# Rounded high and low parts for the query/key norms and the attention scores of a hybrid encoder layer

## The reference

```python
h = rms_norm(x, norm_mix)
proj = h @ w_in                      # fq, fk, fv: 512 columns each, then the other mixers' columns
q = rms_norm(q, q_gain) * (hd ** -0.5)   # per head, over 64 columns
k = rms_norm(k, k_gain)
c = cumsum(log_sigmoid(f_logit))
sc = einsum('bhqd,bhkd->bhqk', q, k) + c[query] - c[key]
p = softmax(where(query >= key, sc, -inf))
o = einsum('bhqk,bhkd->bhqd', p, v)
```

## Time and profile before

| | us |
|---|---|
| median of 3 runs | 872.98 (872.17 to 873.1) |
| the profiled execution | 872.24 |
| its span, first to last instruction | 870.5 |
| PE busy | 840.0 (97%) |
| DVE busy | 579.1 (67%) |
| ACT busy | 475.7 (55%) |

### The profile page before, as it was taken

How to read it: one execution, slowest core, us unless ns; L and a number is a source line. 1 busy time by engine, 2 the same in 40 slices (tenths; PEclk the granted TensorE clock), 3 DMA queues, 4 the chain that set the end, 5 groups by cost and what they waited for, 6 DMA issues and landing times.

```text
span 870.5 us, 11553 instructions
## 1 busy us (share of the span) xinstructions
PE 840.0 (97%) x4188; PEld 673.5 (77%) x4188; DVE 579.1 (67%) x678; ACT 475.7 (55%) x563; POOL 92.2 (11%) x131
## 2 busy tenths in 40 slices
PE   5999999999999989999999999989999999999994
PEld 4777777777877768888888888867888888888883
DVE  5555436766745887324254265788898988889893
ACT  6375445554455242322332332557888788888882
POOL 6510000000000110100000010103112111111001
PEclk9999999999999999999999999999999999999998
DMA  6432012213112031332232494599999999999973
GB/s 213 146 98 72 25 49 98 98 48 98 50 49 97 1 96 49 100 104 97 90 104 97 185 321 164 204 383 347 386 388 369 362 371 377 374 366 352 376 295 49
DMA packets 60173, 164.26 MB, mean 189 GB/s; under 512 B 9592, under 2 KB 10705, under 8 KB 60130
## 3 DMA queue, kind: packets, MB, share of 16 engines
q1 hardware_dynamic: 51504, 145.89, 45.5%
q0 software_dynamic: 4464, 12.66, 6.4%
q10 hardware_dynamic: 4162, 5.13, 1.7%
HBM read 154.16 MB, written 13.11 MB: 192 GB/s over the span
## 4 chain that ended last, share of the span: by engine, by line
PE 90%; DVE 4%; ACT 2%; DMA 1%; issue 1%; POOL 0%; POOLq 0%; DVEq 0%; ACTq 0%
PE bank L1986 26%; PE bank L1988 25%; PE bank L1987 25%; PE bank L2457 1%; PE bank L2108 1%; PE bank L2139 1%; PE bank L2124 1%; DMA xg<-h2rows,tabid 1%; PE bank L2464 1%; PE bank L2096 1%; PE bank L2240 1%; PE bank L2324 1%; PE bank L2190 1%; PE bank L2198 0%; ACT whi L715 0%
## 5 line engine op out<-in xcount | busy, mean ns | idle before, releaser
L737 DVE TENSOR_TENSOR wlo<-mstage,whi 128x2048 fp32r<-128x2048 f32 x95 | 215.5, 2290 | 28.9 <-ACT whi L715 28.8
L715 ACT ACTIVATE whi<-mstage 128x2048 fp32r<-128x2048 f32 x96 | 183.8, 1919 | 25.6 <-PE bank L1988 25.1
L737 DVE TENSOR_TENSOR wlo<-stage,whi 128x2048 fp32r<-128x2048 f32 (+1 forms) x39 | 87.8, 2251 | 96.1 <-ACT whi L715 95.4
L1986 PE MATMUL bank<-hTh,whi 128*128 128x512 f32 x368 | 149.4, 406 | 0.3 <-DVE wlo L1445 0.3
L1988 PE MATMUL bank<-hTh,wlo 128*128 128x512 f32 x368 | 143.7, 390 | 0.0
L1987 PE MATMUL bank<-hTl,whi 128*128 128x512 f32 x368 | 143.4, 390 | 0.0
L715 ACT ACTIVATE whi<-stage 128x2048 fp32r<-128x2048 f32 (+1 forms) x39 | 73.0, 1874 | 75.9 <-PE bank L1988 71.1
L1986 PE MATMUL bank<-whi,xTh 128*128 128x512 f32 (+1 forms) x264 | 104.3, 395 | 2.1 <-DVE xTl L1809 1.1
L1988 PE MATMUL bank<-whi,xTl 128*128 128x512 f32 (+1 forms) x264 | 101.5, 384 | 0.0
L1987 PE MATMUL bank<-wlo,xTh 128*128 128x512 f32 (+1 forms) x264 | 101.2, 383 | 0.0
L1986 PEld LDWEIGHTS bank<-hTh,whi 128*128 128x128 f32 x368 | 69.2, 188 | 17.4 <-issue 2.8
(11 more groups left out here) (383 smaller groups left out, 1333.6 us busy)
## 6 DMA issues: line engine op xcount, KB each, us to landing
mstage<-in_w_exp_gate SPq DMA_DIRECT2D x32, 1024.0 KB, 11.9
mstage<-in_w_exp_up SPq DMA_DIRECT2D x32, 1024.0 KB, 12.0
mstage<-in_w_exp_down SPq DMA_DIRECT2D x32, 1024.0 KB, 12.4
stage<-in_w_in SPq DMA_DIRECT2D x28, 1024.0 KB, 5.0
stage<-in_w_branch SPq DMA_DIRECT2D x6, 1024.0 KB, 5.0
stage<-in_w_out SPq DMA_DIRECT2D x4, 1024.0 KB, 5.1
xin<-in_x SPq DMA_DIRECT2D x4, 512.0 KB, 5.3
x<-in_x SPq DMA_DIRECT2D x4, 512.0 KB, 7.4
```

Of the source, the lines that this page charges most:

```text
L715: nc.scalar.activation(whi_of(u)[:, :, 0:n], source_of(u)[:, :, 0:n], ACT.Copy).then_inc(hi_ready, 1)
L737: nc.vector.tensor_tensor(wlo_of(u)[:, :, 0:n], source_of(u)[:, :, 0:n], whi_of(u)[:, :, 0:n].bitcast(F32), ALU.subtract).then_inc(lo_read ...
L1986: t.matmul(out, lhs[0], rhs[0], start=start, stop=False)
```

## The change

The sums of squares and the scores are made from rounded high and low parts.

1. `square`: ACT, after squaring, also copies the square to a rounded `qsqh`; DVE has a new step that subtracts it from the square (`qsql`) and only then signals `sq_done`. PE multiplies a rounded `blk64r` with both.
2. `parts` m (m = 0 to 7): ACT copies the normed `foxq` or `foxk` to `foxqh` or `foxkh`, DVE subtracts (`foxql`, `foxkl`, in place of the original). Those of the queries stand in the four slots of the second half of block fk, `parts` 4 right behind the last `qscale`, `parts` 5 to 7 in the first three steps of attention.
3. `score`: three matmuls for each head in place of one, in the order high*high, high*low, low*high, each for both heads. The first score of a head pair waits for the key's low part (`ql_done`), the first of all no longer for `qn_done`.
4. POOL makes `blk64r` with one more copy of 128x128. `cum16` moves to another address.

```diff
+    for q in range(4):
+        early.setdefault((1, 1, q), []).append(("parts", q))
...
+                done += [("parts", 4)] if m[0] == 7 else []
...
+        if n < 3:
+            out.append(("parts", 5 + n))
...
+        foxql = at("foxql", 104, [P, 4, T], F32R)
+        foxkl = at("foxkl", 112, [P, 4, T], F32R)
+        foxqh = at("foxqh", 128, [P, 4, T], F32R)
+        foxkh = at("foxkh", 136, [P, 4, T], F32R)
...
-        cum16 = at("cum16", 128, [16, T])
+        cum16 = at("cum16", Z0 + 10, [16, T])
...
+            step(g.tensor_copy(blk64r[:, :], blk64[:, :]))
...
+                elif kind == "parts":
+                    m = it[1]
+                    act.wait_ge(qn_done, m + 1)
+                    step(a.activation((foxqh if m < 4 else foxkh)[:, m % 4, :], (foxq if m < 4 else foxk)[:, m % 4, :],
+                                      ACT.Copy), qh_done, m + 1)
...
-                    step(a.activation(qsq[:, m % 2, :], (foxq if m < 4 else foxk)[:, m % 4, :], ACT.Square),
-                         sq_done, m + 1)
+                    step(a.activation(qsq[:, m % 2, :], (foxq if m < 4 else foxk)[:, m % 4, :], ACT.Square))
+                    step(a.activation(qsqh[:, m % 2, :], qsq[:, m % 2, :], ACT.Copy), sqh_done, m + 1)
...
+                elif kind == "square":
+                    m = it[1]
+                    dve.wait_ge(sqh_done, m + 1)
+                    step(v.tensor_tensor(qsql[:, m % 2, :], qsq[:, m % 2, :], qsqh[:, m % 2, :].bitcast(F32), ALU.subtract),
+                         sq_done, m + 1)
+                elif kind == "parts":
+                    m = it[1]
+                    dve.wait_ge(qh_done, m + 1)
+                    step(v.tensor_tensor((foxql if m < 4 else foxkl)[:, m % 4, :], (foxq if m < 4 else foxk)[:, m % 4, :],
+                                         (foxqh if m < 4 else foxkh)[:, m % 4, :].bitcast(F32), ALU.subtract),
+                         ql_done, m + 1)
...
-                    t.matmul(whole(b), blk64[:, :], qsq[:, m % 2, :], start=True, stop=True).then_inc(full[b], 1)
+                    t.matmul(whole(b), blk64r[:, :], qsqh[:, m % 2, :], start=True, stop=False)
+                    t.matmul(whole(b), blk64r[:, :], qsql[:, m % 2, :], start=False, stop=True).then_inc(full[b], 1)
...
+                    if i == 0:
+                        pe.wait_ge(ql_done, 5 + pr)
                     if n == 0:
-                        pe.wait_ge(qn_done, 8)
                         pe.wait_ge(cuml_done, 2)
-                    for hh, r in enumerate(rows_of):
-                        t.matmul(bank[4 + hh][:, 0:w], foxq[r, pr, i * P:(i + 1) * P], foxk[r, pr, 0:w],
-                                 start=True, stop=False)
+                    for a, b, first in ((foxqh, foxkh, True), (foxqh, foxkl, False), (foxql, foxkh, False)):
+                        for hh, r in enumerate(rows_of):
+                            t.matmul(bank[4 + hh][:, 0:w], a[r, pr, i * P:(i + 1) * P], b[r, pr, 0:w],
+                                     start=first, stop=False)
```

More of the change, by code:

```diff
@@ L445, in build @@
         qsq = at("qsq", Z0, [P, 2, T])
+        qsql = at("qsql", Z0, [P, 2, T], F32R)
+        qsqh = at("qsqh", Z0 + 4, [P, 2, T], F32R)
+        blk64r = at("blk64r", 153, [P, P], F32R)
         qrs = at("qrs", 136, [P, 4, T])
@@ L595, in build @@
             "sq_done", "qrs_done", "qn_done", "min_done", "prob_done", "pv_done", "oAh_done", "tanh_done"))
+        sqh_done = sem("sqh_done")
+        qh_done, ql_done = sem("qh_done"), sem("ql_done")
         sel_done, cumh_done, cuml_done, acsm_done = (sem(n) for n in ("sel_done", "cumh_done", "cuml_done", "acsm_done"))
```

## The result

The change made the kernel slower. The median is 876.76 us (875.65 to 877.56) against 873.04 us for the kernel before in the same job (872.17 to 873.44): +3.7 us, a ratio of 1.0045 (95% interval 1.0035 to 1.0055). The profiled execution took 877.27, its span 875.5 us, 5.0 more than before.

A forecast was written before the change was run, and what follows sets the result against it. PE bounds the kernel, but ACT and DVE hand-overs set its pace up to the first score. Waits 7.1, checks -3.8 and scores -1.9 gave +1.4 on 872.98: 874.4 us, range 871.6 to 877.4.

The forecast's parts named there:

- rival A: The new wait before the first score draws a half-clock stretch of 3.4 us: +1.7, 876.1 us; chance 0.20.
- What bounds the kernel: PE, busy 97% of the span; from 43 to 93.7 us ACT and DVE hand-overs make PE's own savings buy nothing.
- First check: First product for the norm's sums of squares: PE waits for DVE's subtraction, starting at 45.5 not 44.09, +1.4 us.
- Second check: Second norm product: ACT's copy delays the square, subtraction ready 49.75, PE starts 49.9 instead of 48.7, +1.2 us.
- Fifth and seventh: Norm checks where PE waits for DVE's subtraction: fifth (keys) starts 72.3, +1.2 us; seventh starts 79.1, +0.4 us.
- First score: PE waits for DVE's `qscale` and new subtraction behind `bcum`: start 93.7 where it would have come at 90.8, +2.9 us.
- Checks: PE's own work in eight norm checks: two rounded passes, 0.46 us, replace 0.94 us; -3.8 us in all.
- Scores: PE's work in sixteen scores, three rounded products for one float32: -1.0 us by size, -1.9 us with edges.
- half of the edges: In the scores, half of the 0.11 us losses where matmul kinds change would go: -0.9 us.
- B: Scores pay nothing because weight loads lie bare: +3.3 + 1.6, 877.9 us; chance 0.08.
- C: Scores pay best: +3.3 - 3.5, 872.8 us; chance 0.15.
- D: Operands come in time and PE's savings arrive in full: -3.8 - 1.9, 867.3 us; chance 0.09.

The follow-up runs named there:

- the checks alone: The changed kernel with only the norm's checks changed, scores plain float32 and no `parts`; 875.2 us, +2.3 against the kernel before.
- the two kernels that bring the savings back once the chain is covered: The changed kernel with `bcum` behind the second score and splits of units 3, 5, 6 later; queries' `parts` also moved (866.97 us) or left (866.98 us).
- the scores alone: The changed kernel with only the scores changed, all `parts` kept, checks plain float32; 871.46 us, -1.4 against the kernel before.
- `bcum` moved: The changed kernel with the four `bcum` steps on DVE moved behind the second score, nothing else; 872.23 us, 4.5 under the changed kernel.

## Why the prediction was right, and where it was not

The forecast was 874.4 us (+1.4), slower by less than it turned out; the measured 876.76 lies in the range and beside rival A (876.1), which the text gave 0.20. It is in the range because that was drawn to hold A; the forecast's own spread of 1 us does not reach it. Of the signs that were named, three did not come: the second check did not wait for its operand, the fifth waited 0.59 us and not 1 to 2, and the window after 93 us was not at full clock.

- **What bounds the kernel, and that PE's savings ahead of the first score buy nothing:** right. Shown by the checks alone (+2.3 us with 3.8 us less work) and by the two kernels that bring the savings back once the chain is covered.
- **First check:** forecast start 45.5 with 1.4 us more of a wait, measured 45.70 and 1.95 - 0.49 = 1.46.
- **Second check:** the low part was forecast for 49.75 and ended at 49.29 + 0.69 = 49.98. There was no wait of 1.2, because the first check's wait was followed by 3.4 us at half clock (46.1 to 49.6): PE came at 50.57, later than its operand, 2.8 later than before where 2.1 was forecast. In the kernel with the checks alone, whose trace has no such stretch there, the wait was 1.01. So the term came out near its size and with another cause in this trace. What was left of the stretch further on is covered by PE's wait for DVE at the first score. That a wait of 1.95 could draw a stretch stood in rival A only for the first score.
- **Fifth and seventh:** forecast 72.3 and 79.1, measured 72.58 and 79.47; their waits 0.59 and 0.28 against 1.2 and 0.4, since PE itself was later by the half clock.
- **The unit split behind the fourth query slot** (L751) took 3.34 us and not the 2.67 of the same step before, which the forecast did not have (POOL's product on `cumhl` ran beside it for 1.2 us, before for 0.5; the cause was not tested); the `qscale` after it waited 0.26 for ACT and started at 61.11 against 60.9, so it cost nothing.
- **First score:** last `qscale` done at 93.31 against 92.85, start 94.29 against 93.7, wait 2.75 against 2.9; +3.84 in place of +3.3, the rest being 0.15 us by which all of this trace starts later and some 0.05 at each hand-over. That `bcum` stood in this chain was in the working; that the first score does not need it, and that this was the way out, was not said.
- **Checks:** -3.8, with 0.45 us each: right for PE's own work.
- **Scores:** The working has a small slip: a pass at 0.227 us for 512 columns is 0.057 for 128, and 0.053 is a fifth of the slope of 0.267. Slope and floor forecast -1.0, measured 14.71 - 15.73 = -1.0, so this sum came out, with the 128-column score 0.11 longer and the 512-column one 0.16 shorter. The other -0.9, half of the edges, did not come as such (0.2 are gained between the scores). The step failed at "the rows show one such edge in a score and don't tell its owner": the owner is the mask and the score's beginning, which the change doesn't touch.
- **The clock:** this step turned the result in the trace. The mechanism was priced as a rival, at 1.7 us for a stretch of 3.4; "it is shorter than the one that did" was taken as a reason against it. In the trace the stretch was 6.8 us and cost 3.06. Forecast and result differ by 2.3 us in the median: 0.5 from the first score, 0.9 from the edges, and the rest, 0.9, is less than even a short stretch costs; in the single trace the clock counts 3.06 and 0.9 is taken back after 201 us. By the mean granted clocks (0.988 here, 0.990 to 0.992 in the other five executions) the others have some 3 to 7 us less at half clock than this trace. Where it stood in them isn't shown, and the times don't follow these clocks one by one (877.56 at 0.992, 875.65 at 0.990).
- Rivals B and C fall by the scores' own rows, D by the time.

## What to carry to other kernels

When a matmul gets cheaper by means of operands that other engines must prepare, follow the operand's chain first: if PE waits there already, the saving is lost and the added links are paid. Then look through that chain for work that nobody needs yet (here the steps of `bcum` and two splits): moving it turned +3.7 us into -6.0, of which the same moves alone, without the change, give -1.5. And price a new wait of some 2 to 3 us on PE with the half clock that may follow it, not with its length alone.

## What the runs showed of the hardware that was not expected

- **The same wait is followed by different stretches.** PE waits 3.25 us near 310 us (304 to 317) in every one of these kernels. The granted clock in the 20 us from 300, first in the kernel with the scores alone, then with `bcum` moved, then with the checks alone:

```profile
300.00:320.00 20.00, 16.65 (x81) 12.51 (x81) 18.42 (x26) 7.61 (x14) 2.80 (x3) 1.00 0.17 53
```
```profile
300.00:320.00 20.00, 16.66 (x76) 12.75 (x75) 18.39 (x26) 7.88 (x15) 2.79 (x3) 0.91 0.17 53
```
```profile
300.00:320.00 20.00, 16.67 (x68) 12.38 (x68) 18.40 (x28) 7.67 (x14) 2.80 (x3) 0.83 0.16 53
```

  None, 3.4 and 6.8 us at half clock. Of the twelve traces one has none there, five have 3.4 and six 6.8. Against the trace of before, which has 3.4, those with 6.8 lose 1.0 to 1.3 us across this place and the one with none gains 1.3. One trace of one kernel, included, is therefore no price for the next wait. Likewise the wait of 1.95 at 45 us was followed by 3.4 us in after and in the two kernels with `bcum` moved that keep it, and by none with the checks alone. What decides it is open.
- A pair of rounded matmuls of 64 rows and 128 columns, one for each head, starts 0.11 us behind the pair before, no slower than the single ones of 72 columns in the earlier trace rows.
- 0.1 us is lost at the bf16 mask and at the start of a score (0.33 us from one pair of rows to the next in place of 0.23), before and after the change, and nothing between rounded products of the same shape.
